# Layer 1 MLP: six of seven output products deferred by a pair, differences kept in PSUM, weight sums on GpSimd and VectorE

## The reference, cut to what matters

```python
def _sq_relu_mlp(h, w1, w2):
    return jnp.square(jax.nn.relu(h @ w1)) @ w2
...
    h_lat = h_lat + g2 * _sq_relu_mlp(_modulate(_rms_norm(h_lat, norm2_g[i]), sh2, sc2), mlp_w1[i], mlp_w2[i])
```

## Time and profile before

| | before |
|---|---|
| median of 3 runs | 2434.31 us (2430.83 to 2434.5) |
| the profiled execution, its own time | 2434.44 us |
| its span, first to last instruction | 2432.9 us |
| PE busy | 2263.9 us (93%) |
| DVE busy | 1782.4 us (73%) |
| ACT busy | 1158.8 us (48%) |
| POOL busy | 1193.0 us (49%) |

### The profile page before, as it was taken

One profiled execution on the slowest core, in us unless ns is written; L12 is line 12 of the kernel. 1 busy time (PEld: TensorE's weight loads), 2 busy tenths in 40 slices (PEclk: granted clock), 3 DMA queues, 4 the chain that ended last, 5 costly groups with the idle time before them and its releaser, 6 DMA issues. The chain is left out here.

```text
span 2432.9 us, 38281 instructions
## 1 busy us (share of the span) xinstructions
PE 2263.9 (93%) x11430; PEld 1871.9 (77%) x11430; DVE 1782.4 (73%) x2843; ACT 1158.8 (48%) x2133; POOL 1193.0 (49%) x970
## 2 busy tenths in 40 slices
PE   5989979999999999999699799888998999999998
PEld 3768868888888888888587677776776777777777
DVE  5653787777777777777674688881688888888887
ACT  5553443333333333333443588883345554545454
POOL 0003623433333444333646577665636767767674
PEclk9999999999999999999789899999999999999999
DMA  7434213444443345444412211105111212121222
GB/s 269 176 131 175 66 52 104 120 130 116 116 129 103 110 116 137 112 120 120 135 44 104 93 29 40 31 27 190 54 38 49 78 56 74 60 73 57 73 61 83
DMA packets 106153, 234.27 MB, mean 96 GB/s; under 512 B 9424, under 2 KB 18000, under 8 KB 102736
## 3 DMA queue, kind: packets, MB, share of 16 engines
q1 hardware_dynamic: 94432, 209.57, 26.1%
q0 software_dynamic: 8704, 16.78, 4.2%
q10 hardware_dynamic: 2928, 6.82, 0.8%
HBM read 216.35 MB, written 50.33 MB: 110 GB/s over the span
## 5 line engine op out<-in xcount | busy, mean ns | idle before, releaser
L877 POOL TENSOR_TENSOR ht<-ht,l_side 128x512 f32<-128x512 f32 x112 | 150.5, 1344 | 507.4 <-ACT l_side L1004 503.3
L51 PE MATMUL l_z_ps<-nh,l_w1h 128*128 128x512 f32 (+1 forms) x816 | 292.9, 359 | 6.6 <-POOL l_w1l L58 3.4
L53 PE MATMUL l_z_ps<-nh,l_w1l 128*128 128x512 f32 (+1 forms) x816 | 291.7, 358 | 0.0
L52 PE MATMUL l_z_ps<-nl,l_w1h 128*128 128x512 f32 (+1 forms) x800 | 285.7, 357 | 0.0
L1308 DVE SCALAR_TENSOR_TENSOR ht<-l_yy_ps,mod,ht 128x512 f32<-128x512 f32 x336 | 233.9, 744 | 10.9 <-PE l_yy_ps L1624 10.0
L2791 PE MATMUL l_yy_ps<-l_ah,l_w2h 128*128 128x512 f32 x448 | 182.3, 407 | 26.6 <-DVE ht L2582 25.7
L2083 POOL TENSOR_TENSOR ht<-ht,l_side 128x512 f32<-128x512 f32 x112 | 154.2, 1377 | 107.5 <-ACT l_side L2258 106.9
L58 POOL TENSOR_TENSOR l_w2l<-l_w2f,l_w2h 128x512 fp32r<-128x512 f32 x128 | 180.1, 1412 | 33.9 <-ACT l_w2h L2213 30.2
L3520 POOL TENSOR_TENSOR sc<-sc,den 128x640 f32<-128x640 f32 (+1 forms) x128 | 149.5, 1200 | 91.9 <-DVE den L3602 91.9
L58 POOL TENSOR_TENSOR l_w1l<-early,l_w1h 128x512 fp32r<-128x512 f32 x104 | 148.7, 1431 | 77.0 <-ACT l_w1h L2203 77.0
L1622 PE MATMUL l_yy_ps<-l_ah,l_w2h 128*128 128x512 f32 x448 | 178.4, 398 | 6.1 <-DVE ht L1308 6.1
(11 more groups left out here) (339 smaller groups left out, 6486.5 us busy)
## 6 DMA issues: line engine op xcount, KB each, us to landing
l_aw<-ada SPq DMA_DIRECT2D x128, 256.0 KB, 3.0
maw<-ada SPq DMA_DIRECT2D x24, 1024.0 KB, 5.1
l_w1f<-w SPq DMA_DIRECT2D x32, 512.0 KB, 3.8
l_w2f<-w SPq DMA_DIRECT2D x32, 512.0 KB, 4.2
sums<-w SPq DMA_DIRECT2D x32, 512.0 KB, 5.1
sums<-w POOLq DMA_DIRECT2D x32, 512.0 KB, 7.9
early<-w SPq DMA_DIRECT2D x50, 256.0 KB, 2.6
l_w2f<-w SPq DMA_DIRECT2D x48, 256.0 KB, 2.6
```

The costliest lines, as they stand in the source:

```text
L51: pe.matmul(out, lh, rh, start=first, stop=False)
L52: pe.matmul(out, lh, rl, start=False, stop=False)
L53: return pe.matmul(out, ll, rh, start=False, stop=last)
```

## The change

Layer 0 no longer makes weight sums: `start_sums`, `add_sums`, the tensor `sums` and GpSimd's wait for them at the end of the block go. In layer 1 all eight sums of a pair are made on the core: four of w1 on POOL and four of w2 on DVE, from four loaded blocks each. T1, T2 and T4 now lie in PSUM (banks 1 and 2), T3 in SBUF. P1 of a pair is no longer computed in its own pair, but in the next one behind M1, and P2 to P6 each move one hidden product later; pair 1 is deferred too, where it was finished in place before.

```diff
-    DEFERRED = 2
+    W1_SUMS = {1: 1, 2: 2, 4: 3, 5: 4}
+    DEFERRED = {"M1": 1, "M5": 2, "M6": 3, "M2": 4, "M7": 5, "M3": 6}
-    W2_SUMS = {1: 1, 5: 2}
+    W2_SUMS = {4: 1, 1: 2, 2: 3, 5: 4}
-    T_AT = {"T1": 1, "T2": 2, "T3": 3, "T4": 4}
-    HOME_BANK = {"B11": 1, "T4": 1, "T3": 2, "B22": 3}
-    HOME_SLOT = {"T1": 0, "B12": 1, "B21": 2, "T2": 3}
+    T_AT = {"T3": 1, "T2": 2, "T1": 3, "T4": 4}
+    HOME_BANK = {"B11": 1, "T1": 1, "T2": 2, "T4": 2, "B22": 3}
+    HOME_SLOT = {"B12": 1, "B21": 2, "T3": 3}
```

TensorE's list:

```diff
-                def pair(p, earlier=True):
-                    behind = {"M1": 2, "M5": 3, "M6": 4, "M2": 5, "M3": 6}
+                def pair(p):
                     for prod in Z_ORDER:
                         hidden(p, prod)
-                        if earlier and prod in behind:
-                            product(p - 1, behind[prod])
-                    for i in range(DEFERRED):
-                        product(p, i)
+                        if prod in DEFERRED:
+                            product(p - 1, DEFERRED[prod])
+                    product(p, 0)
...
-                for name in ("B11", "B12", "B22"):
+                for name in ("B11", "B12", "B22", "B21"):
                     plain_block(1, (name,))
                 product(1, 0)
-                plain_block(1, ("B21",))
-                for i in range(1, 7):
-                    product(1, i)
-                pair(PLAIN, False)
-                with pe.Fori(PLAIN + 1, PAIRS - 1) as p:
+                pair(PLAIN)
+                with pe.Fori(PLAIN + 1, PAIRS) as p:
                     pair(p)
-                pair(PAIRS - 1)
-                for i in (2, 3):
+                for i in (1, 2, 3):
                     product(PAIRS - 1, i)
```

ScalarE's list, the end of a pair:

```diff
-                    relu(p, "B22")
                     relu(p, "B12")
-                    high(p, "B11")
-                    if earlier:
-                        side_read(p - 1, 6)
+                    side_read(p - 1, 6)
                     high2(p, 2)
                     high(p, "T2")
                     relu(p, "B21")
+                    square_last(p)
                     if more:
                         high1(p + 1, 0)
-                    square_last(p)
                     high(p, "T3")
                     side_read(p, 0)
+                    high(p, "T4")
                     high2(p, 3)
                     if more:
                         high1(p + 1, 2)
-                    high(p, "T4")
-                    high(p, "B21")
-                    side_read(p, 1)
                     high(p, "T1")
-                    high2(p, 4)
-                    high(p, "B22")
```

VectorE's list, the middle and end of a pair, and the sums:

```diff
+                    zsum(p, "B22")
+                    acc(p - 1, 5, (0,))
+                    square(p, "B22")
+                    acc(p - 1, 5, (1, 2, 3))
+                    sum2(p, 4)
                     low2(p, 0)
                     sum2(p, 1)
-                    zsum(p, "B22")
-                    square(p, "B22")
+                    sum2(p, 2)
+                    low(p, "B11")
                     zsum(p, "B12")
...
-                    low(p, "B11")
-                    diff(p, "T1")
-                    diff(p, "T2")
-                    diff(p, "T3")
+                    diffs(p)
                     low(p, "T2")
                     acc(p, 0, (0,))
                     low(p, "T3")
-                    acc(p, 0, (1, 2, 3))
+                    acc(p, 0, (1,))
                     diff(p, "T4")
-                    acc(p, 1)
+                    acc(p, 0, (2, 3))
...
+                def diffs(p):
+                    diff(p, "T3")
+                    diff(p, "T2")
+                    diff(p, "T1")
...
+                    if i == 4:
                         loaded2(dve, p, 4)
+                        loaded2(dve, p, 3)
+                        dve.tensor_tensor(w2f[:, 1], w2f[:, 1], w2f[:, 3], ALU.add).then_inc(s_w2s, 1)
+                    elif i == 1:
                         split2(dve, p, 0)
+                        summed2(dve, p, 4)
+                        dve.tensor_tensor(w2f[:, 0], w2f[:, 0], w2f[:, 1], ALU.add).then_inc(s_w2s, 1)
+                    elif i == 2:
+                        summed2(dve, p, 1)
+                        dve.tensor_tensor(w2f[:, 2], w2f[:, 0], w2f[:, 3], ALU.subtract).then_inc(s_w2s, 1)
```

In pair 2 (`pair(PLAIN, True)`) DVE's list also takes in the twelve `low_t` operations (the low halves of the differences of the tokens T1, T3 and T4) that stood among the outputs of pair 1. Layer 0 loses, at the end of each POOL pair and of the block:

```diff
-                    if C:
-                        add_sums(p, 1)
...
-                if C:
-                    pool.wait_ge(s_sums, 32 * PAIRS)
```

More of the change, by code:

```diff
@@ L1664, in _, with strassen_tail @@
                 outputs(PAIRS - 1, HI_LOOP, out is not None)
-def strassen_tail(nc, sem, sb, banks, wp, early, s_pw, w1, w2, sums, mod, meanw, eps, ident, nh, nl, nl_at, ht, park, out):
+def strassen_tail(nc, sem, sb, banks, wp, early, s_pw, w1, w2, mod, meanw, eps, ident, nh, nl, nl_at, ht, park, out):
     LAYER = 1
@@ L2160, in _ @@
                     add(0, i)
-                for j in range(HK):
-                    low_t("T2", j)
                 low2(1, 1)
+                sum1(2, 1)
                 low1(2, 1)
@@ L2168, in _ @@
                 low2(1, 2)
+                for j in range(HK):
+                    low_t("T2", j)
                 add(1, 0)
@@ L2433, in _ @@
                 pair(last, False)
+                side_read(last, 1)
+                high2(last, 4)
+                high(last, "B21")
+                high(last, "B22")
                 side_read(last, 2)
@@ L2692, in _ @@
                 square(0, "B22")
-                plain_rest(0)
+                diffs(0)
+                low(0, "T2")
+                low(0, "T3")
+                acc(0, 0, (0, 1))
+                diff(0, "T4")
+                acc(0, 0, (2, 3))
+                low(0, "T4")
+                low(0, "T1")
+                acc(0, 1)
+                low(0, "B21")
+                low(0, "B22")
+                acc(0, 2)
+                low2(0, 6)
+                sum2(0, 5)
+                acc(0, 3)
+                low2(0, 5)
+                acc(0, 4)
+                acc(0, 5)
+                acc(0, 6)
+                sum2(1, 4)
                 low2(1, 0)
                 sum2(1, 1)
+                sum2(1, 2)
                 square(1, "B11")
                 low(1, "B11")
-                for one in (third_sum, first_sum, second_sum, fourth_sum):
+                for one in (third_sum, first_sum):
                     for j in range(HK):
@@ L2702, in _ @@
                 square(1, "B12")
+                for j in range(HK):
+                    second_sum(j)
                 square(1, "B22")
-                plain_rest(1)
-                pair(PLAIN, False)
+                diffs(1)
+                low(1, "T2")
+                for j in range(HK):
+                    fourth_sum(j)
+                low(1, "T3")
+                acc(1, 0, (0, 1))
+                diff(1, "T4")
+                acc(1, 0, (2, 3))
+                pair(PLAIN, True)
                 with dve.Fori(PLAIN + 1, PAIRS) as p:
                     pair(p)
-                pair_start(PAIRS)
-                acc(PAIRS - 1, 5)
-                acc(PAIRS - 1, 6)
+                last = PAIRS - 1
+                low(last, "T4")
+                low(last, "T1")
+                acc(last, 1)
+                low(last, "B21")
+                low(last, "B22")
+                acc(last, 2)
+                low2(last, 6)
+                sum2(last, 5)
+                acc(last, 3)
+                low2(last, 5)
+                for i in (4, 5, 6):
+                    acc(last, i)
                 for i in range(len(HALVES)):
```

308 lines of the change are left out of this document (113 added, 195 removed).

## The result

The changed kernel takes 2479.82 us (median of 4 runs, 2478.04 to 2481.25) against 2434.4: a ratio of 1.019, 95% interval 1.0178 to 1.0202. It is slower, 45.4 us by the medians, where +48 was forecast.

The account below looks back on a forecast made before the run. PE was taken to bound layer 1's loop, with M1 newly waiting for its weight. Loop +52.4, start -3, tail +4 and end of layer 0 -5.3 gave +48 on 2434.44, thus 2482 us, range 2446 to 2496.

Parts of the forecast that it names:

- twelve periods: Layer 1's loop from pair 3 on: each period 44.1 us against 39.73, 4.37 more, +52.4 in all.
- end of layer 0: After layer 0's MLP: PE no longer waits for the weight sums' DMA and goes on at 1188.1, -5.3 us.
- start, to M1 of pair 3: Pairs 1 to 3: in-place waits go, tokens' low halves load DVE in pair 2; -3 us, bounds -9 and +3.
- tail, from M1 of pair 15: Behind the last pair: one more product and three outputs back to back behind DVE; +4 us, +1 to +7.
- What bounds the kernel and what M1 hangs on: Layer 1's loop: PE bounds; M1 needs w1's low half on POOL, thus its high half on ACT, queued behind T2's.
- The walk: End of a pair, timed from M7's first matmul: T2 at 15.9, M1 at 20.2 instead of 16.56, a 3.6 us wait.
- DVE stands for POOL: End of a pair: POOL blocks DVE's low half of w2 until near 8.8 and its second sum until 10.55.
- The clock: PE behind M1's wait in every pair: matmuls fall to the 1.2 GHz level, costing 1.7 us each time.
- the rival in which the clock stays up: Loop: one block instead of two, or no clock loss; period 42.4, total 2462, range 2445 to 2470; 27%.
- The square ahead of the high half: ACT, end of a pair: B21's square now stands ahead of w1's high half, adding 0.55 us to M1's chain.
- P1's slot: Between M4 and M1: without P1 the cover loses 2.76 plus 1.1 of wait, 3.8 us, from a 3.26 reserve.
- The faster rival: Loop: M1 hangs only on M4's end if T2 is there by t = 14; period 39.5, about 2421 to 2429; 8%.

Follow-up runs that it names:

- Run 1: Changed kernel with only ACT's order altered: relu of B21 and the next pair's high half of w1 ahead of T2's high half; 2430.6 us.
- run 4: Changed kernel with two POOL operations per pair, the add of P5' and a low half of w1, cut to 64 columns; 2449.17 us.
- run 5: Changed kernel with DVE's second and third w2 sums in the loop cut to 64 columns; 2457.37 us.
- run 6: Changed kernel with ACT's square of B21 put back behind the high half of the next pair's first weight block; 2464.39 us.
- run 2: Changed kernel with P1 back in its own pair behind P0, sums and differences as changed; 2489.21 us.
- run 8: Changed kernel with layer 0's weight sums and the wait for them put back, though nothing reads them; 2485.19 us.
- 10: Kernel of run 9 with relu and square of B21 in pair 1 also ahead of T2's high half on ACT; 2425.81 us.
- 12: Kernel of run 9 with DVE's low half of T3 after P0's accumulations and T4, and pair 1's relu and square of B21 early; 2416.39 us.
- run 9: Kernel of run 1 with POOL's low half of the next pair's w1 also ahead of its low half of w2 for P2; 2426.67 us.
- 3: Changed kernel with P1 back in its own pair and DVE's accumulation of P0's second bank ahead of T3's low half; 2490.18 us.

## Why the prediction was right, point by point

The times of M1 split the 46.5 us between the two profiled spans. Before, M1 of pair 3 is at 1886.17 and that of pair 15 here:

```profile
2362.68 0.39 PE L2774 MATMUL l_z_ps<-nh,l_w1h 128*128 128x512 f32 x1
```

After:

```profile
2404.42 0.49 PE L2736 MATMUL l_z_ps<-nh,l_w1h 128*128 128x512 f32 x1 [3.38 <-POOL l_w1l L58]
```

| term | forecast | measured |
|---|---|---|
| twelve periods | +52.4 | 522.69-476.51 = +46.2 |
| end of layer 0 | -5.3 | 1188.18-1193.46 = -5.3 |
| start, to M1 of pair 3 | -3 | 1881.73-1886.17+5.28 = +0.8 |
| tail, from M1 of pair 15 | +4 | 74.98-70.22 = +4.8 |
| sum | +48 | +46.5 |

The total is nearer than its parts. The loop was put 6.2 too high and the start 3.8 too low; that these two partly cancel is luck. The direction and the mechanism are not.

- **What bounds the kernel and what M1 hangs on**: shown. Run 1 changes nothing but who stands ahead of the high half of w1 on ACT, and 49 us go, with the period back at 39.75 (39.71 before).
- **The walk**: right to 0.3 us at every step. Its period without the clock, 42.4, is 42.31 in the trace.
- **DVE stands for POOL**: shown by runs 4 and 5, in which a sum of an eighth of the width takes 1.20 us. The Trainium skill's rule (page "SBUF — State Buffer", section "Who interferes with whom"), that the engine which starts second is blocked until the other's instruction ends, agrees with this row. That POOL's operations get longer too was not in the walk.
- **The clock** is the mis-sized term: 1.7 was put on every pair. Measured, it is 1.56 in eight of twelve (43.87 against 42.31), 2.4 in one, and nothing in three: 1.25 on average, 12 x 0.45 = 5.4 of the 6.2 by which the loop was overestimated. For those three pairs the rival in which the clock stays up was right.
- **The square ahead of the high half**: it was taken as 0.55 and is worth 0.65 of wait, but 15 us in all (run 6), because the clock then falls in four periods of twelve and not in nine. Why it falls less often was not tried.
- **P1's slot**: the prediction's argument that it was part of what hid the chain holds for M1 (run 2: no wait at M1), but it didn't say that the same lateness would be paid at P1 in its old place. To undo that part alone is worse than the change.
- **Layer 0**: the mechanism holds, and run 8 confirms it from the other side. The join, taken as 1.3, is 1188.18-1186.94 = 1.24. That the term agrees to the tenth is luck: in the eleven other kernels with this layer 0 TensorE goes on at 1186.74 to 1188.96, which is -4.5 to -6.7.
- **The start** came out 3.8 above the forecast, inside its bounds: the waits of pair 1 went, and 7.5 ahead of pair 2's M1, 2.5 for the tokens' low halves and 3.4 at pair 3 took their place. The last of these is nearly the whole miss: the walk gives thirteen pairs such a wait, but the sum has twelve periods from M1 of pair 3 on, so the wait ahead of that M1 stood in no term. Runs 10 and 12 show that the 7.5 is no loss of its own.
- **The tail**: inside its bounds. Of its 4.8, some 1.6 are the clock's fall behind the wait at pair 15 (matmuls at 0.63 from 2404.75 to 2408.29), which no term had either.
- **The faster rival** ("T2 there by t = 14") was argued from DVE's idle time and did not come. The time it named was reached in another way (run 9), by making M1 independent of T2.

Of the forecasts for the runs, those of 2, 3, 5, 6 and 9 failed. In run 2 the order of DVE was left out, in 3 and 6 the clock was misjudged, in 5 a blocked sum was priced by its own size, and in 9 I took M1's wait as the last one, when DVE's reads of P0's banks were next behind it.

## What to carry to other kernels

When a product is moved to another place, find what ran behind it: the slot may have been the cover of a chain on other engines, and every queue's order was written for the old place. Look at the in-order queues of that chain for an instruction that waits for something which the chain itself does not need (here the high half of T2 ahead of the next weight's high half); to move it cost nothing and was worth 49 us, while to trim the work that made it late gave 22 to 31. Reorder the other queues until the last wait is gone, and time each step, for each removes only the wait that ended last.

## What was not expected of the hardware

- The same wait does not always lower TensorE's clock: behind 3.4 us the matmuls of nine pairs in twelve went to 0.63 (the 1.2 GHz level, pitch 0.43) for a while and those of three stayed at 0.39. Over the runs the share grows with the wait: none of thirteen behind 0.8 us (run 1), one of twelve behind 1.95 (run 4), four of twelve behind 2.48 (run 5), five of twelve behind 2.7 (run 6, pairs 4 to 15). Each count is from one profiled execution.
- Two short waits near each other can cost more clock than a long one. Behind 1.87 us, with 0.78 more shortly after, the matmuls stayed at 0.63 from 2013.26 to 2019.95, 6.7 us with the second wait in it, where behind 3.4 us it was mostly eight matmuls in some 3.4 us. Why it stayed so long was not tried.
- A DVE instruction of 64 columns can take 1.20 us: its time in the trace is that of the POOL instruction it stands behind.
